# The last batch of expert gates kept in its staging buffer, gate quads spread over more tiles, and rings of four for the rounded activations

## The chip, the cores and the metric

The kernel runs on one core of one Trainium2 chip. The metric is the time of the whole kernel on the device, in microseconds (us). Time before: 3241.5 us, the median of 3 runs (3241.14 to 3247.5).

## The reference

Two decoder layers over 512 tokens of width 1024. Each ends in a mixture of single-neuron experts (128 x 128 = 16384 of them) with 8 retrieval heads that pick 16 experts each for every token. Only this part is touched by the change:

```python
def peer_ffn(h, w_query, sub_keys1, sub_keys2, expert_u, expert_v):
    ...
    gate = jax.nn.softmax(top_v.astype(jnp.float32), axis=-1).astype(h.dtype)
    ...
    def block(args):
        xt, et, gt = args
        act = jax.nn.gelu(jnp.einsum("td,thkd->thk", xt, expert_u[et]), approximate=False) * gt
        return jnp.einsum("thk,thkd->td", act, expert_v[et])
```

## The kernel before

Experts are not gathered for the first 384 of the 512 tokens. For these the kernel computes all experts densely: `a[e, t] = gelu(u_e . h_t) * G[e, t]`, where `G` holds the gates (zero for experts that were not picked), and then `y_t = sum_e a[e, t] v_e`. The last 128 tokens (`FETCHED`) fetch their 128 rows of `u` and `v` each. One layer thus has three stages that matter here.

- **U tiles.** `U` is streamed in 128 tiles (number `n`) of 128 experts. A tile is 24 matmuls on PE (`u_tile`, L948 to L950): 8 slices of the width, each with three products, since weights and activations are split into a rounded high part and a low part. ACT rounds the weight tile (`high`, L500), POOL or DVE subtracts to get the low part (`low`, L437 or L1694), ACT applies gelu (L684) into `gel`, a ring of four, and stores it to DRAM (L688). PE alternates between two banks, so tile `n` waits for the gelu of tile `n - 2`. The last `KEPT = 4` tiles' gelus stay in `gel`.
- **Gates, beside the U tiles from tile `U_EARLY = 26` on.** The gates of four tokens at a time (a quad, 96 of them) are made by DVE's one-hot tiles `hot` and `plane` (L1703, L1708), ACT's low planes (`low_planes`, L723), 4 matmuls on PE (`gate_quad`, L1201), and two adds that put the result in `stage` (`gates_high` on ACT, L733, and `gates_out` on DVE, L1717). `quad_step(q)` says before which of the 8 slices of which tile PE does quad `q`; ACT and DVE take the same table: in tile `n` they finish the quads that PE does there, and prepare the quad two further on. Twelve quads are a batch of 48 tokens. `stage` has two slots of 24 KB in each partition. When a batch is complete, ACT stores it to `g_dram` in four pieces (`store_piece`, L740), one after each of four U tiles; the last batch's four pieces go out together.
- **Rows of the fetched tokens.** POOL fetches rows of `u` (`u_fetch`, L454) and DVE takes the dot product of each with the token (`dot`, L1726), 5 in 4 tiles. Until `U_GATED` POOL also does `low` of tile `n + 2`; from there DVE does.
- **V tiles.** After tile `FIRST_UNIT_AT`, ACT waits until all stored gates have landed and loads the first two units (`load_unit`, L749 and L752): a unit is the gates and the gelus of four tiles. Then, three tiles ahead of PE (`V_AHEAD`), DVE multiplies gelu by gate (`product`, L1754), ACT rounds the product (`a_high`, L760) and DVE subtracts (`a_low`, L1763), into `a_hi` and `a_lo`, rings of 8; PE does 18 matmuls for a V tile (L968). Per V tile DVE also does `low` and adds one fetched row of `v` (L1741).

Every engine works through its own list in order. ACT's list for one U tile, in this order: `high` of tile `n + 3`; for each quad of the tile `gates_high(q)` and `low_planes(q + 2)`; the gelu and its store; a piece of a batch; the first units if it is their turn. DVE's list: for each quad `one_hots(q + 2)` and `gates_out(q)`, then the dots. A wait at the head of a list holds all that is behind it.

## Time and profile before

| | us |
|---|---|
| median of 3 runs | 3241.5 |
| lowest and highest | 3241.14, 3247.5 |
| the profiled execution | 3235.31, span 3233.6 |

PE is busy 95% of the span, DVE 83%, ACT 47%, POOL 50%; the mean granted TensorE clock is 0.979. The DMA engines moved 846.06 MB, 262 GB/s over the span. A view by windows gives each engine's busy time in a stretch, the granted clock and the share of time in which the DMA engines were busy. Rows of waits read "who waited <- for what: us in total, times, longest"; rows of a timeline read start, duration, engine, line, operation, result and sources, and in brackets how long the engine sat idle before and what ended it. The first layer's U tiles with quads run from 565 to 1009 us, its remaining U tiles to 1069, its V tiles to about 1595; the second layer's from 2206 to 2642, to 2701 and to about 3223.

### The profile page before, as it was taken

How to read it: one execution, taken by the hardware profiler on the slowest of the kernel's cores; microseconds unless marked ns; L12 is line 12 of the kernel's file. 1: busy time of each engine (PE TensorE's matmuls, PEld its weight loads, DVE VectorE, ACT ScalarE, POOL GpSimd, SP SyncE). 2: the span in 40 equal slices, each digit the busy share in tenths (PEclk: the TensorE clock that was granted, in tenths of full speed). 3: DMA queues.
4: the chain of work that ended last, by engine and by line, in shares of the span. 5: the costliest groups of instructions: out<-in, count | busy, mean ns of one | idle time of the engine just before them, and what ended most of it. 6: DMA issues, size and time to landing. Idle time of an engine off the chain costs nothing.

```text
span 3233.6 us, 44817 instructions
## 1 busy us (share of the span) xinstructions
PE 3082.8 (95%) x15340; PEld 2681.0 (83%) x15340; DVE 2699.0 (83%) x4632; ACT 1506.1 (47%) x2678; POOL 1617.0 (50%) x880
## 2 busy tenths in 40 slices
PE   4899999999998999999899998999999998999999
PEld 3777799999998888878677667899999997888887
DVE  6676898999997888888875658997999987798887
ACT  3233334666664333333444763346666753333332
POOL 3423345898786443444333004457898884552221
PEclk9899999999999999999999899999999999999999
DMA  5533235899899999999624013257999999999996
GB/s 217 200 134 108 76 115 183 285 343 334 322 317 375 365 368 357 382 360 378 237 79 156 1 39 128 96 164 245 323 345 338 354 355 356 360 366 355 355 351 247
DMA packets 321829, 846.06 MB, mean 262 GB/s; under 512 B 26753, under 2 KB 155793, under 8 KB 321505
## 3 DMA queue, kind: packets, MB, share of 16 engines
q1 hardware_dynamic: 90448, 329.82, 28.7%
q0 software_dynamic: 74000, 268.81, 22.6%
q10 hardware_dynamic: 157184, 244.88, 20.9%
q8 instruction: 117, 1.92, 0.2%
q14 instruction: 80, 0.65, 0.1%
HBM read 742.20 MB, written 101.19 MB: 261 GB/s over the span
## 4 chain that ended last, share of the span: by engine, by line
PE 56%; DVE 19%; POOL 9%; DMA 7%; issue 6%; ACT 1%; ACTq 1%; DVEq 0%; POOLq 0%; SPq 0%
PE banks L968 19%; PE gbank L968 9%; DVE u_rows L1726 7%; POOL w_lo L437 6%; DVE hot L1703 4%; POOL u_rows L454 3%; PE banks L928 3%; PE banks L930 3%; PE banks L929 3%; PE banks L948 3%; PE banks L950 3%; PE banks L949 3%; DMA u_rows<-u_dram,row_of 3%; DVE plane L1708 2%; DVE stage L1717 2%
## 5 line engine op out<-in xcount | busy, mean ns | idle before, releaser
L437 POOL TENSOR_TENSOR w_lo<-raw,w_hi 128x1024 fp32r<-128x1024 f32 x339 | 833.3, 2460 | 783.1 <-ACT w_hi L500 779.8
L500 ACT ACTIVATE w_hi<-raw 128x1024 fp32r<-128x1024 f32 x613 | 648.2, 1058 | 541.0 <-PE banks L968 305.0
L948 PE MATMUL banks<-h_hi,w_hi 128*128 128x384 f32 x2048 | 696.2, 340 | 44.8 <-ACT gel L684 39.1
L462 POOL DMA_INDIRECT v_rows<-v_dram,row_of x256 | 403.4, 1576 | 615.8 <-DVE fetched L1741 599.8
L949 PE MATMUL banks<-h_lo,w_hi 128*128 128x384 f32 x2048 | 688.2, 336 | 0.0
L950 PE MATMUL banks<-h_hi,w_lo 128*128 128x384 f32 x2048 | 688.1, 336 | 0.0
L1726 DVE CUSTOM_DVE_ANT_0 u_rows<-u_rows,h_rows 128x1024 f32<-128x1024 f32 x256 | 462.6, 1818 | 35.6 <-DMA u_rows<-u_dram,row_of 35.5
L454 POOL DMA_INDIRECT u_rows<-u_dram,row_of x256 | 372.1, 1454 | 188.1 <-DVE z L1726 154.1
L948 PEld LDWEIGHTS banks<-h_hi,w_hi 128*128 128x128 f32 x2048 | 387.2, 189 | 61.9 <-issue 46.4
L949 PEld LDWEIGHTS banks<-h_lo,w_hi 128*128 128x128 f32 x2048 | 387.1, 189 | 0.0
L950 PEld LDWEIGHTS banks<-h_hi,w_lo 128*128 128x128 f32 x2048 | 386.7, 189 | 0.0
L1694 DVE TENSOR_TENSOR w_lo<-raw,w_hi 128x1024 fp32r<-128x1024 f32 x274 | 333.8, 1218 | 12.4 <-ACT w_hi L500 12.4
L1741 DVE SCALAR_TENSOR_TENSOR fetched<-v_rows,share,fetched 128x1024 f32<-128x1024 f32 x254 | 326.6, 1286 | 1.2 <-DMA v_rows<-v_dram,row_of 0.7
L723 ACT ACTIVATE plane<-hot,gate_lo 128x128 fp32r<-128x128 f32 x768 | 246.2, 391 | 168.6 <-DVE hot L1703 151.9
L968 PE MATMUL banks<-w_hi,a_lo 128*128 128x512 f32 x1024 | 315.3, 389 | 0.0
L968 PE MATMUL banks<-w_hi,a_hi 128*128 128x512 f32 x1024 | 315.2, 389 | 0.0
L968 PE MATMUL banks<-w_lo,a_hi 128*128 128x512 f32 x1024 | 315.2, 389 | 0.0
L928 PE MATMUL banks<-h_hi,w_hi 128*128 128x512 f32 x696 | 285.2, 410 | 1.4 <-DVE h_lo L1863 1.4
L760 ACT ACTIVATE a_hi<-gin 128x384 fp32r<-128x384 f32 x248 | 129.0, 520 | 330.3 <-DVE gin L1754 324.6
L930 PE MATMUL banks<-h_hi,w_lo 128*128 128x512 f32 x696 | 272.5, 392 | 0.0
L929 PE MATMUL banks<-h_lo,w_hi 128*128 128x512 f32 x696 | 272.5, 392 | 0.0
L1703 DVE TENSOR_TENSOR hot<-banks,exT 128x1024 fp32r<-128x1024 f32 x192 | 233.2, 1215 | 1.0 <-PE gbank L1201 0.9
(320 smaller groups left out, 4862.1 us busy)
## 6 DMA issues: line engine op xcount, KB each, us to landing
raw<-stream_dram SPq DMA_DIRECT2D x613, 512.0 KB
g_dram<-stage ACTq DMA_DIRECT2D x64, 768.0 KB
gates<-g_dram ACTq DMA_DIRECT2D x64, 768.0 KB
gel_dram<-gel ACTq DMA_DIRECT2D x248, 192.0 KB
gin<-gel_dram ACTq DMA_DIRECT2D x62, 768.0 KB
ada_w<-ada_dram ACTq DMA_DIRECT2D x50, 512.0 KB
ada_out<-ada_dram ACTq DMA_DIRECT2D x18, 512.0 KB, 4.6
ada_first<-ada_dram SPq DMA_DIRECT2D x8, 1024.0 KB, 20.0
```

Of the source, the lines that this page charges most:

```text
L437: pool.tensor_tensor(w_lo[:, s, :], raw[:, s, :], w_hi[:, s, :].bitcast(F32), ALU.subtract).then_inc(split_lo, 1)
L454: pool.indirect_dma_start(u_rows[:, j % U_ROWS, :], None, (u0, u1)[layer], bass.IndirectOffsetOnAxis(ap=row_of[:, j:j + 1], axis=0)).then_ ...
L462: pool.indirect_dma_start(v_rows[:, j % V_ROWS, :], None, (v0, v1)[layer], bass.IndirectOffsetOnAxis(ap=row_of[:, j:j + 1], axis=0)).then_ ...
L500: act.activation(w_hi[:, s, :], raw[:, s, :], ACT.Copy).then_inc(split_hi, 1)
L928: pe.matmul(out, wh, hi(k), start=(k == 0), stop=False)
L929: pe.matmul(out, wh, lo(k), start=False, stop=False)
L930: mm = pe.matmul(out, wl, hi(k), start=False, stop=(k == DC - 1))
L948: pe.matmul(out, wh, h_hi[:, k, 0:DENSE_T], start=(k == 0), stop=False)
L949: pe.matmul(out, wh, h_lo[:, k, 0:DENSE_T], start=False, stop=False)
L950: mm = pe.matmul(out, wl, h_hi[:, k, 0:DENSE_T], start=False, stop=(k == DC - 1))
L968: mm = pe.matmul(sums[c][half][:], a, w[:, half * SEQ:(half + 1) * SEQ], start=(v == 0 and a is ah and w is hi), stop=(v == NKEYS - 1 and ...
L1726: dve.tensor_tensor_reduce(row, row, h_rows[:], 1.0, 0.0, ALU.mult, ALU.add, z[:, j:j + 1]).then_inc(S("dotted"), 1)
```

## The change

1. Only the first 7 of the 8 batches are stored and loaded (`STORED`). The eighth stays in slot 1 of `stage`, and `product` becomes two instructions: 336 elements by the loaded gates, and 48 by `stage[:, 1, expert]`. For the first product DVE waits for its own last `gates_out`.
2. To leave slot 1 alone, `gates` and `gin` fit in slot 0 and `a_hi`, `a_lo` move behind `stage`, where the one-hots are before; their rings shrink from 8 to 4.
3. `quad_step` steps by 49/6 slices in place of 15/2. The last quad is in tile 124 in place of 116, so `U_GATED` is 125 in place of 117, and POOL does `low` for 8 more tiles. The batches are complete in tiles 39, 51, 64, 76, 88, 100 and 113 in place of 38, 50, 61, 72, 83, 95, 106 (and 117). Before, tiles 35, 50, 65, 80, 95 and 110 hold two quads each; now none does, and tiles 51 and 100 hold none.
4. The first units are loaded after tile 120 in place of 121, and so while quads still run.

```diff
-A_RING = 8
+A_RING = 4
...
+STORED = NBATCH - 1
+REST = STORED * BATCH
...
-    return QUAD_FROM + 15 * q // 2
+    return QUAD_FROM + 49 * q // 6
...
-FIRST_UNIT_AT = U_GATED + 4
+FIRST_UNIT_AT = NKEYS - 8
...
-    gates = sb("gates", [P, 2, NBATCH, UNIT, BATCH])
+    gates = sb("gates", [P, 2, STORED, UNIT, BATCH])
     gin = sb("gin", [P, 2, UNIT, DENSE_T])
+    place[0] = arena + 2 * NKEYS * BATCH * 4
...
-            batch_at = {quad_step(BATCH_QUADS * b + BATCH_QUADS - 1) // DC + 1: b for b in range(NBATCH)}
+            batch_at = {quad_step(BATCH_QUADS * b + BATCH_QUADS - 1) // DC + 1: b for b in range(STORED)}
...
-                    if n - i in batch_at and (i == 0 or batch_at[n - i] < NBATCH - 1):
+                    if n - i in batch_at:
                         store_piece(batch_at[n - i], i)
-                if batch_at.get(n) == NBATCH - 1:
-                    for i in range(1, PIECES):
-                        store_piece(NBATCH - 1, i)
                 if n == FIRST_UNIT_AT:
                     for s in range(2):
-                        act.wait_ge(S(f"stored{s}"), past[f"stored{s}"] + 16 * PIECES * ((NBATCH + 1 - s) // 2))
+                        act.wait_ge(S(f"stored{s}"), past[f"stored{s}"] + 16 * PIECES * ((STORED + 1 - s) // 2))
...
-                dve.tensor_tensor(x.rearrange("p (b t) -> p b t", b=NBATCH),
-                                  x.rearrange("p (b t) -> p b t", b=NBATCH),
-                                  gates[:, u % 2, :, j, :], ALU.mult).then_inc(S("product"), 1)
+                if n == 0:
+                    dve.wait_ge(S("g_out"), past["g_out"] + QUADS)
+                loaded = x[:, 0:REST].rearrange("p (b t) -> p b t", b=STORED)
+                dve.tensor_tensor(loaded, loaded, gates[:, u % 2, :, j, :], ALU.mult)
+                dve.tensor_tensor(x[:, REST:], x[:, REST:], stage[:, STORED % 2, (n - KEPT) % NKEYS, :],
+                                  ALU.mult).then_inc(S("product"), 1)
```

The lines of the kernel after are numbered 1 to 4 higher from here on. DVE's list at the first tile with two quads (tile 35; `hot` and `plane` prepare a quad, `stage` finishes one, the rows named u_rows and z are a dot), before:

```order
L1703 TENSOR_TENSOR hot<-banks,exT 128x1024
L1708 TENSOR_TENSOR plane<-hot,banks 128x4x128
L1717 TENSOR_TENSOR stage<-stage,gbank 128x128x4
L1703 TENSOR_TENSOR hot<-banks,exT 128x1024
L1708 TENSOR_TENSOR plane<-hot,banks 128x4x128
L1717 TENSOR_TENSOR stage<-stage,gbank 128x128x4
L1726 ISA u_rows,z<-u_rows,h_rows 128x1024
L1726 ISA z 128x1
```

The same place now:

```order
L1704 TENSOR_TENSOR hot<-banks,exT 128x1024
L1709 TENSOR_TENSOR plane<-hot,banks 128x4x128
L1718 TENSOR_TENSOR stage<-stage,gbank 128x128x4
L1727 ISA u_rows,z<-u_rows,h_rows 128x1024
L1727 ISA z 128x1
L1704 TENSOR_TENSOR hot<-banks,exT 128x1024
L1709 TENSOR_TENSOR plane<-hot,banks 128x4x128
L1718 TENSOR_TENSOR stage<-stage,gbank 128x128x4
```

The second quad has moved behind the dots, into the next tile.

ACT's list around the load of the first units, from the `high` of tile 121 on, before:

```order
L500 ACTIVATE w_hi<-raw 128x1024
L684 ACTIVATE gel<-banks 128x384
L688 DMA gel_dram<-gel 128x384
L749 DMA gates<-g_dram 128x8x192 x2
L752 DMA gin<-gel_dram 128x4x384
L500 ACTIVATE w_hi<-raw 128x1024
L684 ACTIVATE gel<-banks 128x384
```

Now, from the quad of tile 120 on:

```order
L737 ACTIVATE stage<-gbank 128x128x4
L727 ACTIVATE plane<-hot,gate_lo 128x128 x4
L688 ACTIVATE gel<-banks 128x384
L692 DMA gel_dram<-gel 128x384
L753 DMA gates<-g_dram 128x7x192 x2
L756 DMA gin<-gel_dram 128x4x384
L504 ACTIVATE w_hi<-raw 128x1024
L737 ACTIVATE stage<-gbank 128x128x4
L727 ACTIVATE plane<-hot,gate_lo 128x128 x4
L688 ACTIVATE gel<-banks 128x384
```

The three loads now stand in front of a tile with a quad: its two quad steps (`stage`, `plane`) are behind the loads and ahead of the gelu that PE waits for.

## Rows read from the trace of the kernel before

**Rows 1.** Windows: us, each engine's busy us (and instructions), granted clock, DMA share, GB/s.

```profile
565.00:1009.00 444.00, 427.73 (x2526) 419.94 (x2525) 432.83 (x504) 296.35 (x654) 374.28 (x200) 0.99 0.91 323
1009.00:1069.00 60.00, 49.08 (x264) 47.68 (x263) 36.27 (x49) 17.67 (x25) 25.70 (x17) 0.91 0.96 367
1069.00:1592.00 523.00, 520.34 (x2293) 430.29 (x2294) 441.83 (x548) 194.55 (x256) 224.94 (x131) 1.00 0.96 366
2206.00:2642.00 436.00, 424.88 (x2529) 416.37 (x2528) 426.13 (x504) 296.69 (x654) 377.28 (x200) 1.00 0.92 329
2642.00:2701.00 59.00, 48.23 (x262) 46.86 (x260) 35.68 (x49) 17.15 (x25) 25.18 (x17) 0.91 0.97 371
```

**Rows 2.** Timeline of PE: three gate quads in tiles 102, 103 and 104.

```profile
939.38 0.64 PE L1201 MATMUL gbank<-plane,hot 128*128 128x256 f32 x4
943.50 0.64 PE L1201 MATMUL gbank<-plane,hot 128*128 128x256 f32 x4
948.14 0.64 PE L1201 MATMUL gbank<-plane,hot 128*128 128x256 f32 x4
```

**Rows 3.** Waits of PE from 565 to 1009 us, the largest.

```profile
PE banks L948 <- ACT gel L684: 11.9, 9, 3.4
```

**Rows 4.** Waits of PE from 2206 to 2642 us, the largest.

```profile
PE banks L948 <- ACT gel L684: 8.5, 9, 2.6
```

**Rows 5.** Timeline of ACT in tile 35, the first with two quads.

```profile
606.53 1.28 ACT L723 ACTIVATE plane<-hot,gate_lo 128x128 fp32r<-128x128 f32 x4 [1.82 <-issue]
```

**Rows 6.** Timeline of PE behind it.

```profile
610.78 0.41 PE L948 MATMUL banks<-h_hi,w_hi 128*128 128x384 f32 x1 [1.35 <-ACT gel L684]
```

**Rows 7.** Waits of PE from 990 to 1075 us.

```profile
PE banks L948 <- ACT gel L684: 9.2, 1, 9.2
PE banks L948 <- DVE w_lo L1694: 1.0, 1, 1.0
```

**Rows 8.** Waits of PE from 2620 to 2706 us.

```profile
PE banks L948 <- ACT gel L684: 9.5, 1, 9.5
```

**Rows 9.** Timeline of ACT around the first units of the first layer.

```profile
1031.87 0.34 ACTq L688 DMA_DIRECT2D gel_dram<-gel  x1
1034.71 7.21 ACTq L749 DMA_DIRECT2D gates<-g_dram  x2
1041.94 5.39 ACTq L752 DMA_DIRECT2D gin<-gel_dram  x1
```

**Rows 10.** Timeline of ACT later, the load of one unit among the V tiles.

```profile
1107.81 0.37 ACTq L749 DMA_DIRECT2D gates<-g_dram  x1
1108.21 0.61 ACTq L752 DMA_DIRECT2D gin<-gel_dram  x1
```

**Rows 11.** DMA queues from 1034 to 1048 us, ACT's own: packets, MB, share of 16 engines.

```profile
q10 hardware_dynamic: 1150, 1.16, 23.2%
```

**Rows 12.** Timeline of ACT: the gelu of tile 102.

```profile
944.64 0.47 ACT L684 ACTIVATE gel<-banks 128x384 f32<-128x384 f32 x1
```

**Rows 13.** Windows, columns as in rows 1: the first 5 us after the stall.

```profile
1049.00:1054.00 5.00, 4.99 (x16) 5.00 (x17) 5.00 (x7) 2.49 (x3) 2.24 (x2) 0.50 1.09 396
```

**Rows 14.** Timeline of DVE: two dots in tile 102.

```profile
944.65 1.98 DVE L1726 CUSTOM_DVE_ANT_0 u_rows<-u_rows,h_rows 128x1024 f32<-128x1024 f32 x1
...
946.56 1.22 DVE L1726 CUSTOM_DVE_ANT_0 u_rows<-u_rows,h_rows 128x1024 f32<-128x1024 f32 x1
```

**Rows 15.** Timeline of POOL at that time.

```profile
943.12 2.42 POOL L437 TENSOR_TENSOR w_lo<-raw,w_hi 128x1024 fp32r<-128x1024 f32 x1
945.70 1.76 POOL L454 DMA_INDIRECT u_rows<-u_dram,row_of  x1 [0.16 <-issue]
```

**Rows 16.** The product's line: duration in ns, least, median and most.

```profile
L1754 DVE TENSOR_TENSOR gin<-gin,gates x248: 545/551/560, 1075.8 to 3206.5; 128x384 f32<-128x384 f32 x124
```

**Rows 17.** Timeline of DVE: the nearest small multiply, 96 elements.

```profile
1073.09 0.25 DVE L1734 TENSOR_TENSOR share<-share,z 128x96 f32<-128x96 f32 x1
```

**Rows 18.** Waits of PE from 1069 to 1600 us, the largest.

```profile
PE gbank L968 <- DVE w_lo L1694: 2.5, 1, 2.5
```

More of the change, by code:

```diff
@@ L115 @@
 COUNTS = {"scores": N_WQ, "sc": N_WQ, "ranked": N_WQ, "gate_arg": 1, "gate_exp": 1, "ex": 3, "ex_tp": 3,
-          "exT": 5, "hot": QUADS, "one": QUADS, "one_lo": QUADS, "gate_lo": 1, "g_mm": QUADS, "g_hi": QUADS, "g_out": QUADS, "stored0": 16 * PIECES * ((NBATCH + 1) // 2), "stored1": 16 * PIECES * (NBATCH // 2), "picked": 2,
+          "exT": 5, "hot": QUADS, "one": QUADS, "one_lo": QUADS, "gate_lo": 1, "g_mm": QUADS, "g_hi": QUADS, "g_out": QUADS, "stored0": 16 * PIECES * ((STORED + 1) // 2), "stored1": 16 * PIECES * (STORED // 2), "picked": 2,
           "h_rows": 1, "h_copied": 1, "v_row": 16 * PICKS // V_ROWS, "dotted": PICKS, "z_gel": 2,
@@ L328, in build @@
     fetched = sb("fetched", [P, D])
-    g_dram = [nc.dram_tensor(f"g_dram{l}", (NBATCH, P, NKEYS, BATCH), F32, kind="Internal").ap()
+    g_dram = [nc.dram_tensor(f"g_dram{l}", (STORED, P, NKEYS, BATCH), F32, kind="Internal").ap()
               for l in range(2)]
```

## The prediction

> **What bounds the kernel now.** I read the windows by stage first. In the V tiles PE is busy 520.3 of 523 us at full clock [rows 1]: PE alone bounds them, and the DMA engines' 96% and DVE's 442 us are cover that is almost used up but still covers. The waits of PE say so too: one of 2.5 us in the first layer's V tiles [rows 18]. The two stretches of U tiles are where time can move: 444 and 436 us for tiles 27 to 116, 60 and 59 us for the rest [rows 1].
>
> What would PE alone need? The quads at 939.38, 943.50 and 948.14 are 7 and then 8 slices apart [rows 2]: 4.12 and 4.64 us. So a slice (3 matmuls) is 0.52 us, a tile 4.16, a quad 4.12 - 7 x 0.52 = 0.48. Ninety tiles with 96 quads are 374.4 + 46.1 = 420.5 us. The stretches took 444 and 436: 23.5 and 15.5 us over. The eleven tiles behind are 45.8 us of matmuls in 60 and 59 us: 14.2 and 13.2 over. These four excesses, 66.4 us in all, are what the change can touch; the rest of the kernel is as it was.
>
> **Part 1: no tile with two quads.** In tile 35 ACT's first plane of a quad starts 1.82 us late, since DVE has two quads' one-hots to make in one tile and ACT's gelu stands behind both planes; PE then waits 1.35 us for that gelu [rows 5, 6]. PE waited for a gelu 9 times in each stretch, 11.9 and 8.5 us [rows 3, 4]. By their times those behind tiles 35, 50, 65, 80, 95 and 110 add up to 5.9 us in each layer. Each such wait costs a little more than it shows, since the first matmul behind it takes 0.41 us where it starts the next after 0.17 when PE runs on; with about 8 waits that is 1.9. Sum: 7.8 us in a layer. Some would remain (the wait at tile 65 has a late fetched row in it too), so I take 7.5 off, between 4 and 9. The quads themselves are not removed: 96 x 0.48 is paid in either table. What is late next is the loop of POOL and DVE: POOL's low part, then a fetch, then the next low part [rows 15]: 2.42 + 0.16 + 1.76 is 4.34 in a tile with one dot, and one tile in four has a second dot, 1.22 us at the least [rows 14]: 4.65 on average, against PE's 4.64. So the cover behind PE is thin, and what I take off cannot be more than the 9.
>
> **Part 2: the last batch's store goes.** After tile 117 its four pieces crowd the DMA engines; PE waits 1.0 us for a low part whose weights came late [rows 7]. Off: 1.0 in a layer, down to nothing if it was chance. The seven other batches are stored as before, only 12.25 tiles apart in place of 11.25, so their collisions with late rows stay: no change, with 3 us to either side in a layer, since they fall on other tiles.
>
> **Part 3: the first units.** Before, ACT ended tile 121 at 1032.2, waited 2.5 us for the store to land, and then was held by three loads for 7.21 + 5.39 = 12.6 us; PE stood for 9.2 us [rows 7, 9], 9.5 in the second layer [rows 8]. (a) The wait for the store goes: the last stored piece now leaves after tile 116, four tiles earlier. That is 2.5 off. (b) The loads still hold ACT. One unit later on costs 0.37 + 0.61 us [rows 10], so not the issue itself is slow but the queue is full: gates are 1024 pieces of 768 bytes, gin 512. In 14 us the queue passed 1150 packets [rows 11], 82 in a us; 12.6 us are 1030, the size of one load of gates. I read it as: the third load gets in when as much as the first one has left. Three loads are now 896 + 896 + 512, 256 fewer: 12.6 - 256 / 82 = 9.5 us, 3.1 off. Bounds: nothing off (the hold is a time and no count), and 7 us left (the queue drains faster, with no store before it). (c) Against it, the place is worse. Where quads run, ACT's gelu lags: tile 103's quad is at slice 3 and at 943.50, so tile 102 had ended at 941.9, and its gelu came at 944.64 [rows 2, 12], 2.7 us late, where after tile 121 it was at once. Behind the loads ACT now does a stage copy and four planes ahead of the gelu: 0.6 + 1.3. PE's two tiles of slack are longer by two quads: 1.0. Sum: 9.2 - 2.5 - 3.1 + 2.7 + 1.9 - 1.0 = 7.2 us, 2.0 less than before, between 5 and 10, the bounds of (b). (d) After the stall PE runs at 0.50 of its clock (the 1.2 GHz level) for 16 matmuls in 5 us [rows 13], 2.3 us lost; that stays. (e) DVE stands too, at the stage add of tile 121, while PE's list behind has three more quads. I add 1.0 for it, between 0 and 3.
>
> **Part 4: eight tiles more with POOL's low part.** A dot beside POOL's subtraction takes 1.98 us, and one beside a fetch 1.22 [rows 14, 15]: in tiles 117 to 124 ten dots are 7.6 us longer, but DVE no longer makes these tiles' low parts, and at one quad a tile it keeps PE's pace as it does in tiles 51 to 113. PE pays at most 0.03 a tile by that loop, and I add 0.3 for a stray wait: 0.5 in a layer, between 0 and 3. The Trainium skill (SBUF — State Buffer, on the pair of ports that DVE and GpSimd share) says that a DVE instruction with two SBUF inputs and a GpSimd one that reads SBUF exclude each other for the whole instruction; the 1.98 beside 1.22 agrees with it.
>
> **Part 5: the V tiles.** The product of 384 elements takes 0.551 us [rows 16]; the nearest small multiply, 96 elements, 0.25 [rows 17]. Two instructions for one cost between 0 and 0.25 us more; I take 0.1, 12 us of DVE's time in a layer, where DVE is idle for 523 - 442 = 81 [rows 1]. Off the path. The unit's gates are 96 KB less, and land sooner. The only spot where DVE was late is the 2.5 us [rows 18]: 0, between -2.5 and +3. The Trainium skill (VectorE: DVE Perf Modes, the TRN2 errata on a fixed latency per instruction) speaks against the split: by its formula for an fp32 tensor_tensor, (N + 151) cycles at 0.96 GHz, the two are 0.16 us more than the one; by it DVE would lose 20 us in a layer, still inside the 81. The rings of four cost nothing: ACT rounds product v + 3 only behind its weight rounding, which has already waited for PE's tile v - 1.
>
> **Sum** in a layer: -7.5 - 1.0 - 2.0 + 1.0 + 0.5 = -9.0 us; two layers -18.0. By its own time the profiled execution would go from 3235.3 to 3217.3; the median shown is 6.2 above that execution, and I forecast against it: 3241.5 - 18.0 = 3223.5 us.
>
> **The rivals.** (A) The quads' stalls move and do not go. The two-quad waits are what pays, and with so thin a cover the POOL and DVE loop may be late elsewhere, once a fetched row is late. Then -7.5 becomes -2, and the stall at the loads stays as long as it was: -2 - 1.0 + 1.0 + 0.5 = -1.5 a layer, 3238.5. For it: DVE is busy 433 of 444 us; against it: the long waits stand exactly behind the two-quad tiles in both layers. (B) The queue takes the three loads at once, since they are fewer: PE's stall goes with its slow clock, another 7.2 + 2.3 + 1.0 a layer: 3202.5. Against it: in the first layer two loads, 2048 pieces, were already held for 7.2 us [rows 9], and now the three are 2304. (C) Slower. The loads come while DVE still has quads and dots; rows arrive late, and ACT's planes wait for DVE in each tile from 121 to 124, and DVE comes into the V tiles behind. Its price: the worst gelu wait among the quads, 3.4 us [rows 3] with another 2.3 of slow clock [rows 13], once or twice in a layer; with Part 1 half paid and Part 3 at nothing: -4 - 1.0 + 1.0 + 5.7 x 1.5 + 0.5 = +5.1 a layer, 3251.7. It decides from the point where DVE is more than 12.5 us (the three tiles 125 to 127) behind PE at tile 124. Against it: behind the quads DVE is busy for only 36 of 60 us [rows 1], so it catches up fast. (D) The change does nothing at the loads and the two-quad waits were no more than 4: near A.
>
> **Chances.** Forecast 0.70, with its own range 3212 to 3233; A (with D) 0.17; B 0.06; C 0.07. A measurement of this kernel can tell about 0.2% (6.5 us) from no change. Faster than 3235: the forecast, B and a small part of A: 0.76. Same: 0.17. Slower: 0.07. The range takes in A's time and leaves out most of B and C: 3211 to 3240.
>
> **What the profile after would show.** PE's waits for a gelu from 565 us to tile 124: under 7 us in a layer, and none behind tiles 35, 50, 80, 95 and 110; the gelus of these tiles 4.3 to 5.6 us apart like their neighbours. The three loads after tile 120 hold ACT for 9 to 10 us, with no wait in front, and PE stands once for about 7 us, then 16 or so matmuls at 0.50. V begins about 9 us earlier, counted from the first quad. The V tiles take 523 us again. It would be wrong if PE's waits in tiles 26 to 116 are as long as before (A), or PE waits more than once behind tile 120 (C), or not at all (B).

## The result

The kernel after takes 3202.2 us (median of 4 runs, 3198.4 to 3210.0) beside 3244.5 us (3241.1 to 3261.4) for the kernel before on the same chip: ratio 0.986, 95% interval 0.984 to 0.989, some 44 us less. On another chip it came to 0.989 (0.986 to 0.993). The forecast was 18 us less, and the time lies below its range. Ratios here are of fast runs alone; the one slow run among all kernels took 6172 us (e10_before_ring4 below), and why is not known. The profiled execution of after took 3201.2 us, with a mean granted clock of 0.982 in place of 0.979.

Windows of the kernel after by stage, columns as in [rows 1]: the first layer's U tiles with quads up to the loads of the first units, the rest of its U tiles, its V tiles, and the two U stretches of the second layer.

```profile
559.00:1010.00 451.00, 441.89 (x2641) 437.03 (x2641) 431.65 (x510) 299.43 (x654) 401.34 (x210) 1.00 0.92 333
1010.00:1044.00 34.00, 28.73 (x159) 28.13 (x159) 28.03 (x35) 15.72 (x28) 24.37 (x14) 0.95 0.93 326
1044.00:1582.00 538.00, 528.62 (x2304) 435.62 (x2304) 455.59 (x680) 196.67 (x259) 262.55 (x130) 0.99 0.94 352
2191.00:2633.00 442.00, 438.66 (x2632) 435.29 (x2631) 422.82 (x509) 298.84 (x651) 404.49 (x210) 1.00 0.94 339
2633.00:2667.00 34.00, 30.46 (x168) 29.56 (x166) 27.65 (x36) 16.23 (x31) 25.48 (x15) 0.95 0.95 337
```

From the first quad to the first V tile it is 484.7 and 476.3 us, before 505.3 and 496.4: some 20 us less in each layer, not 9. Against that the first layer's V tiles, forecast at 523 again, take 538.7 after and 526.6 before; the second layer's take 523.4 in both. Another 4.4 us came ahead of the first quad (563.7 and 559.3 us), where no instruction differs; later executions of either kind start their quads anywhere from 557 to 566 us, so this is chance.

Waits of PE in the kernel after, columns as in [rows 3]: U tiles up to the loads, U tiles from there, V tiles; then the second layer's U tiles in the same two parts.

```profile
PE banks L949 <- ACT gel L688: 6.8, 3, 2.6
...
PE banks L949 <- ACT gel L688: 3.8, 1, 3.8
...
PE gbank L969 <- DVE w_lo L1695: 8.7, 4, 3.3
...
PE banks L949 <- ACT gel L688: 2.4, 1, 2.4
...
PE banks L949 <- ACT gel L688: 2.3, 1, 2.3
```

The nine waits for a gelu among the quads in each layer [rows 3, 4] are three and one, as forecast. The stall of 9.2 and 9.5 us at the loads [rows 7, 8] was to be 7.2; it is 3.8 and 2.3. What DVE's low parts cost in the V tiles has grown from 2.5 us [rows 18] to 8.7.

ACT's timeline of after at the loads, the first layer, then the second. Rows of ACTq are DMA issues; their duration is how long the issue kept ACT.

```profile
1010.07 1.21 ACTq L753 DMA_DIRECT2D gates<-g_dram  x2
1011.31 4.28 ACTq L756 DMA_DIRECT2D gin<-gel_dram  x1
...
2634.56 1.12 ACTq L753 DMA_DIRECT2D gates<-g_dram  x2
2635.71 0.71 ACTq L756 DMA_DIRECT2D gin<-gel_dram  x1
...
2639.64 3.94 ACTq L692 DMA_DIRECT2D gel_dram<-gel  x1
```

Three loads held ACT for 12.6 us before [rows 9]. Now it is 5.5 us in the first layer; in the second the loads go in within 1.9 us, and the next gelu's store is held for 3.9. The first load starts 0.6 us behind the gelu's store: ACT no longer waits for stored gates.

The queues of after from 1010 to 1016 us: packets, MB, share of 16 engines.

```profile
q10 hardware_dynamic: 1036, 0.87, 45.8%
q0 software_dynamic: 68, 0.22, 9.4%
```

ACT's queue q10 passed 1036 packets in 6 us, 173 in a us, where it had passed 82 [rows 11]. Before, q0, which brings the fetched rows, had 52.9% of the engines in the 14 us of [rows 11]; here it has 9.4%.

PE's clock behind the stall, two windows of after: the last 3 us of the stall and the 5 us behind.

```profile
1016.00:1019.00 3.00, 0.09 (x1) 0.12 (x2) 1.74 (x2) 2.77 (x7) 2.17 (x1) 1.00 1.04 386
1019.00:1024.00 5.00, 5.00 (x22) 5.00 (x23) 4.97 (x8) 3.62 (x8) 1.12 (x2) 0.66 1.05 409
```

After 3.8 us idle the clock is at 0.66 over 5 us, where 9.2 us idle had brought 0.50 [rows 13]: 22 matmuls in place of 16. In the second layer 2.3 us idle brought 0.66 from 2648 to 2653 us as well. While PE was at work the slow clock cost 2.5 us before (5 us at 0.50) and 1.7 after (5 us at 0.66).

### The profile page after: what moved, and what is told of

Its sections match the earlier page's. It is cut to its first block, busy times and chain, and to the rows that moved or that the text cites. A ratio compares the mean times of both kernels' runs of the same rounds, so it can differ in the third digit from the quotient of the medians.

```text
span 3199.2 us, 45065 instructions
## 1 busy us (share of the span) xinstructions
PE 3071.2 (96%) x15340; PEld 2678.8 (84%) x15340; DVE 2703.6 (85%) x4872; ACT 1504.9 (47%) x2678; POOL 1653.5 (52%) x896
## 4 chain that ended last, share of the span: by engine, by line
PE 51%; POOL 23%; issue 9%; DVE 9%; DMA 7%; ACT 1%; ACTq 0%; POOLq 0%; DVEq 0%; SPq 0%
PE banks L969 17%; POOL w_lo L441 14%; POOL u_rows L458 9%; PE gbank L969 8%; DMA ada_w<-ada_dram 4%; PE banks L929 3%; PE banks L931 3%; PE banks L930 3%; DVE u_rows L1727 2%; PE banks L950 2%; PE banks L951 2%; PE banks L949 2%; DMA u_rows<-u_dram,row_of 2%; DVE w_lo L1695 1%; DVE hot L1704 1%
## 5 line engine op out<-in xcount | busy, mean ns | idle before, releaser
L441 POOL TENSOR_TENSOR w_lo<-raw,w_hi 128x1024 fp32r<-128x1024 f32 x355 | 870.4, 2454 | 775.9 <-ACT w_hi L504 769.9
L466 POOL DMA_INDIRECT v_rows<-v_dram,row_of x256 | 390.4, 1525 | 645.6 <-DVE fetched L1742 630.3
L458 POOL DMA_INDIRECT u_rows<-u_dram,row_of x256 | 384.6, 1502 | 95.3 <-DVE z L1727 52.6
L1695 DVE TENSOR_TENSOR w_lo<-raw,w_hi 128x1024 fp32r<-128x1024 f32 x258 | 314.0, 1217 | 0.0
## 6 DMA issues: line engine op xcount, KB each, us to landing
gin<-gel_dram ACTq DMA_DIRECT2D x62, 768.0 KB, 13.3
```

The lines of the kernel that those rows point to most:

```text
L441: pool.tensor_tensor(w_lo[:, s, :], raw[:, s, :], w_hi[:, s, :].bitcast(F32), ALU.subtract).then_inc(split_lo, 1)
L458: pool.indirect_dma_start(u_rows[:, j % U_ROWS, :], None, (u0, u1)[layer], bass.IndirectOffsetOnAxis(ap=row_of[:, j:j + 1], axis=0)).then_ ...
L466: pool.indirect_dma_start(v_rows[:, j % V_ROWS, :], None, (v0, v1)[layer], bass.IndirectOffsetOnAxis(ap=row_of[:, j:j + 1], axis=0)).then_ ...
```

## The experiments

For each profiled execution I took two excesses: the time between the gelus of two tiles, less 4.16 us a tile and 0.48 a quad, the needs of PE worked out in the prediction. One is over tiles 27 to 116, the other over 116 to 127, where the loads are. "Gelu" means its start on ACT. "U" is first quad to first V tile, "V1" the first layer's V tiles. Two numbers are the two layers. Ratios are to the kernel before, with 95% intervals.

| kernel | ratio | U | excess 27 to 116 | excess 116 to 127 | V1 |
|---|---|---|---|---|---|
| before | 1 | 505.3, 496.4 | 24.2, 15.8 | 13.6, 13.1 | 526.6 |
| before_again | 1.000 (0.998 to 1.003) | 500.0, 497.7 | 19.2, 17.5 | 13.3, 12.7 | 535.7 |
| after | 0.986 (0.984 to 0.989) | 484.7, 476.3 | 13.9, 6.7 | 3.3, 2.1 | 538.7 |
| after_again | 0.989 (0.986 to 0.993) | 480.8, 478.4 | 10.8, 8.5 | 2.5, 2.4 | 531.4 |
| e1_old_spread | 0.992 (0.990 to 0.995) | 490.7, 497.3 | 17.4, 21.7 | 5.7, 8.0 | 532.2 |
| e5_burst | 0.999 (0.997 to 1.001) | 497.6, 500.3 | 18.4, 19.0 | 11.6, 13.7 | 544.6 |
| e9_burst_no_wait | 0.999 (0.997 to 1.001) | 502.8, 496.4 | 20.8, 14.6 | 14.3, 14.2 | 537.8 |
| e4_two_quads | 0.987 (0.983 to 0.991) | 483.9, 486.5 | 13.7, 15.6 | 2.6, 3.4 | 541.4 |
| e6_twelve_two_quads | 0.993 (0.990 to 0.996) | 482.3, 487.2 | 15.5, 17.3 | -0.8, 2.4 | 539.5 |
| e8_every_tile | 0.988 (0.985 to 0.992) | 483.3, 474.2 | 9.2, 5.5 | 6.4, 1.2 | 543.0 |
| e2_one_product | 0.987 (0.983 to 0.990) | 477.4, 478.5 | 9.9, 11.3 | 0.0, -0.3 | 527.1 |
| one_product_again | one run, 3212.3 us | 484.6, 488.4 | 14.7, 18.2 | 2.3, 2.7 | 535.8 |
| e3_dot_later | 0.982 (0.978 to 0.987) | 481.4, 489.4 | 9.2, 16.0 | 4.7, 5.9 | 524.9 |
| e7_split_loads | 0.985 (0.981 to 0.988) | 480.8, 478.6 | 10.8, 11.5 | 2.5, -0.5 | 525.0 |
| before_split_loads | 0.998 (0.996 to 1.000) | 501.9, 492.4 | 23.1, 13.4 | 11.3, 11.4 | 533.8 |
| e10_before_ring4 | 1.000 (0.998 to 1.003) | 505.8, 499.5 | 24.2, 18.2 | 13.9, 13.8 | 542.8 |
| e11_before_dot_later | 0.995 (0.994 to 0.997) | 499.6, 500.1 | 18.4, 19.2 | 13.7, 13.4 | 523.4 |
| e12_sum | 0.982 (0.979 to 0.984) | 477.1, 468.0 | 10.1, 3.3 | -0.6, -2.9 | 525.0 |

One execution's U tiles differ by several us from the next with the same program, so means count. In tiles 27 to 116 the old table's eight kernels (the two of before, e1, e5, e9, before_split_loads, e10, e11) have a mean excess of 19.1 us a layer, the 49/6 table's six (the two of after, e2, e3, e7, one_product_again) one of 11.8: 7.3 us less, with some 2.5 to either side by their scatter.

These two excesses have a fault: they end at the gelu of tile 116, and how late that gelu is depends on the table. The old table has no more quads to prepare there, so ACT runs the gelu 0.2 us behind PE's end of the tile in all 16 layers; with the new table it comes 2.8 to 6.9 us behind. First PE's quad in tile 115 before and in tile 116 after, then the gelus of tile 116, before and after:

```profile
1002.07 0.63 PE L1201 MATMUL gbank<-plane,hot 128*128 128x256 f32 x4
...
980.00 0.64 PE L1202 MATMUL gbank<-plane,hot 128*128 128x256 f32 x4
```

```profile
1008.95 0.49 ACT L684 ACTIVATE gel<-banks 128x384 f32<-128x384 f32 x1 [1.49 <-PE banks L950]
...
990.44 0.47 ACT L688 ACTIVATE gel<-banks 128x384 f32<-128x384 f32 x1
```

So I also took the excess on PE itself, by its quads: from the first quad to the last one up to slice 931 (slice 925 with the old table, 930 with the new, both about tile 116), less 0.52 us a slice and 0.48 a quad, and from there to the first V tile. Means over the layers:

| kernels | first quad to tile 116 | tile 116 to V |
|---|---|---|
| before's order: old table, a last store, loads after tile 121 (before, before_again, e5, e9, e10, e11; 12 layers) | 21.6 | 14.4 |
| e1_old_spread: old table, no last store, loads after tile 120 | 22.0 | 7.8 |
| after's order: new table, no last store, loads after tile 120 (after, after_again, e2, e3, one_product_again; 10 layers) | 9.6 | 8.3 |
| e4_two_quads | 14.9 | 6.2 |
| e6_twelve_two_quads | 17.2 | 3.4 |
| quads every 8 slices (e8_every_tile, e12_sum) | 6.5 | 5.0 |

The split moves: up to tile 116 the new table saves 11.8 us a layer (21.5 in the old table's eight kernels, 9.7 in the new one's six; 2.3 to either side), and from there to V the change saves 6.2 (2.2 to either side), where the gelus gave 7.3 and 10.8. The sum is the same 18. PE's idle time up to tile 116 fell from 13.0 to 5.7 us a layer, and its waits of any length from 17 to 6.

### The table and the last store

Theory: the new table makes most of the gain. Rival: that the last batch is not stored does.

```diff
-    return QUAD_FROM + 49 * q // 6
+    return QUAD_FROM + 15 * q // 2
```

> The changed kernel with the old table of quads (steps of 15/2 slices: six tiles with two quads, last quad in tile 116), the rest of the change kept: seven batches stored, loads after tile 120. Theory 1 (the spread pays by having no tile with two quads, the missing store pays at the loads): 8 to 10 us a layer come back in tiles 27 to 120, so about 3218 us; the loads hold ACT for 5 to 6 us, as in the changed kernel, and PE stands for less than 4 us there. Theory 2 (the spread is worth nothing, all of the gain is the store that went): 3200 to 3204 us. Theory 3 (all of it is the spread): PE stands 7 us or more at the loads again, 3235 or more.

The old table gives back about half of the gain. Its excess up to tile 116 is that of before. Behind it the excess stays some 6 us below before. The burst was put back onto this kernel, in four pieces behind the last quad, with ACT's wait for it ahead of the loads:

```diff
-FIRST_UNIT_AT = NKEYS - 8
+FIRST_UNIT_AT = NKEYS - 7
...
+                if n == U_GATED:
+                    act.wait_ge(S("g_out"), past["g_out"] + QUADS)
+                    for i in range(PIECES):
+                        own = slice(i * NKEYS // PIECES, (i + 1) * NKEYS // PIECES)
+                        act.dma_start(burst_dram[layer][:, own].rearrange("p e t -> p (e t)"),
+                                      stage[:, STORED % 2, own, :].rearrange("p e t -> p (e t)")
+                                      ).then_inc(S("burst"), 16)
                 if n == FIRST_UNIT_AT:
+                    act.wait_ge(S("burst"), past["burst"] + 16 * PIECES)
```

> The changed kernel with the old table of quads, and with the eighth batch stored after tile 117 in four pieces at once, to a tensor that nobody reads, and waited for in front of the first loads, which are after tile 121: so all is as in the kernel before, but for the loads of seven batches (2304 pieces of data, not 2560) and the split product. Theory R (the loads are held for a count of packets, and what changed is the rate at which ACT's queue drains, since after a burst of stores the late rows take the DMA engines): the loads hold ACT for 8 to 11 us again and PE stands 6 to 9 us in a layer; 12 us more than with the old table of quads alone, 3236 to 3244. Theory C (the fewer pieces alone do it): they hold ACT for 5 us, PE stands less than 5 us, 3226 to 3232.

With table, store and the place of the loads as before, the time is that of before, and so is nearly the stall (8.4 and 9.2 us). These three are the change, as far as time goes; the 256 fewer pieces to load and the split product aren't told from nothing. To see whether the wait or the hold makes the stall, the same kernel had the wait moved behind the U tiles:

> The kernel of run e5_burst (old table, eighth batch stored in four pieces behind tile 117, units loaded after tile 121) without ACT's wait for that store ahead of the loads; the wait stands behind the U tiles now. There the wait was 3 us and the three loads held ACT for 12.3 and 11.7 us, and PE stood 8.4 and 9.2. Theory (the queue lets ACT go when so many packets have left, whatever they are): the loads enter a queue that still holds the rest of the store, so they hold ACT longer by what the wait was, 14 to 16 us in all; PE stands 8 to 9.5 us as in e5_burst, U tiles 497 to 500 us, the whole time the same within 0.3%. Rival (the forecast's sum: wait and hold add up): the hold stays at 12, PE stands 5.5 to 6.5 us, U tiles 494 to 497 us, 5 us off the whole time.

ACT's loads in e5_burst (first layer), then in e9_burst_no_wait (both layers):

```profile
1025.20 4.61 ACTq L755 DMA_DIRECT2D gates<-g_dram  x2
1029.84 7.69 ACTq L758 DMA_DIRECT2D gin<-gel_dram  x1
```

```profile
1029.23 8.04 ACTq L755 DMA_DIRECT2D gates<-g_dram  x2
1037.30 6.91 ACTq L758 DMA_DIRECT2D gin<-gel_dram  x1
...
2674.25 1.06 ACTq L755 DMA_DIRECT2D gates<-g_dram  x2
2675.34 14.21 ACTq L758 DMA_DIRECT2D gin<-gel_dram  x1
```

12.3 us of hold behind a wait became 15.0 and 15.3 without one, PE stood 9.3 and 9.7 us (8.4 and 9.2 in e5_burst), and the time is the same. So while the store is in the queue, wait and hold are one thing: without the wait ACT spends the same time on the issue. It does not say that the store makes the hold: in e5_burst the store had landed before the loads were issued, and they were held for 12.3 and 11.7 us all the same.

In e1_old_spread, with no store in the queue, the loads held ACT like this, first layer and second:

```profile
1020.19 1.31 ACTq L753 DMA_DIRECT2D gates<-g_dram  x2
1021.52 7.93 ACTq L756 DMA_DIRECT2D gin<-gel_dram  x1
...
2660.79 1.20 ACTq L756 DMA_DIRECT2D gin<-gel_dram  x1
...
2663.56 11.30 ACTq L692 DMA_DIRECT2D gel_dram<-gel  x1
```

Four tiles behind the last quad the holds are still 9.2 us, and 2.8 and then 11.3 (PE stands 3.8 and 6.1 us), with q10 at 140 packets in a us from 1021 to 1030 and 91 from 2660 to 2675, and q0 at 39 to 47% of the engines. My expectation was 5 to 6 us of hold and under 4 of stall, so Theory 1 held only in part. From tile 116 to V the excess is 14.4 us with the store and its wait, 7.8 without them, and 8.3 in after's order, where the loads stand beside the quads. So by this the 6.2 us there go with the store and the wait for it, and the place beside the quads cost next to nothing. That rests on the two layers of e1_old_spread, 6.7 and 8.9.

Nor is the hold of 5.5 us in after's first layer the rule for this program. In eight of the ten layers with after's order the three loads went in within 2.5 us, and in four of these eight the next store of a gelu was then held, for 2.4 to 6.9 us; PE stood for 0 to 5.2 us, 1.8 on average, where it stood for 8.4 to 10.7 in the twelve layers with before's order. ACT's loads in after_again, first layer:

```profile
1013.17 1.33 ACTq L753 DMA_DIRECT2D gates<-g_dram  x2
1014.52 0.82 ACTq L756 DMA_DIRECT2D gin<-gel_dram  x1
```

In all kernels with the new table q0 had 3 to 43% of the engines while the loads went in, in those with the old one 36 to 53%. Why the fetched rows leave more room beside the quads isn't shown; that PE asks for a weight tile every 4.64 us there and every 4.16 behind the quads is only argued.

### What in the table pays

Theory: the tiles with two quads. They were put back into the new table alone, by moving the quads of six tiles one tile ahead, then of twelve:

```diff
-    return QUAD_FROM + 49 * q // 6
+    step = QUAD_FROM + 49 * q // 6
+    if step // DC in TWO_QUADS:
+        step = step // DC * DC - 1
+    return step
+
+
+TWO_QUADS = (36, 45, 66, 81, 90, 111)
```

> The changed kernel with six quads moved back to the last slice of the tile in front (tiles 36, 45, 66, 81, 90 and 111 lose theirs to the tile before), so that six tiles have two quads again, while the last quad is still in tile 124. Theory 1 (a tile with two quads costs PE 1.3 to 1.6 us): 8 to 10 us a layer, 3218 to 3222. Theory 2 (such tiles cost nothing, fewer quads in a tile on average is what pays): 3200 to 3205.

> The changed kernel with twelve tiles of two quads (the quads of tiles 31, 36, 41, 45, 58, 66, 73, 81, 86, 90, 104 and 111 in the last slice of the tile in front), twice the dose of the run with six. Theory 1 (1.3 to 1.6 us for each such tile): 16 to 19 us a layer more than the changed kernel, 3233 to 3240. Theory 3 (about 0.6 us each, as the run with six says within its noise): 7 us a layer, 3216 to 3220. Theory 2 (nothing): 3202.

> The kernel after with one thing changed: the quads' table steps by 8 slices in place of 49/6, so that every tile from 27 on has exactly one quad and the last is in tile 122. By the five earlier executions with the new table, tiles 27 to 116 take 11 us more than PE's matmuls need, with the old table 19, and with six or twelve tiles of two quads put into the new one 15 to 16. Theory: two-quad tiles make up half of the difference and the denser table (7.5 slices a quad, so 1.25 dots and more than one quad to a tile for DVE) the other half. 8 slices is as free of two-quad tiles as the new one and three quarters as wide: 11 to 14 us over in tiles 27 to 116, U tiles 480 to 487 us, whole time within 0.3% of the kernel after (ratio to before 0.985 to 0.990). Rival: only the two-quad tiles count; then 9 to 12 us over, and the U tiles as after. Rival: the rare tile without a quad (two in the new table) is where a late DVE gets back; without any, a delay is never caught up: over 17 us, U tiles over 488.

Waits of PE among the quads, first layer: e6_twelve_two_quads, then e12_sum (a quad every 8 slices, below) in the second layer.

```profile
PE banks L955 <- ACT gel L694: 8.3, 8, 3.7
```

```profile
PE banks L950 <- ACT gel L688: 0.9, 1, 0.9
PE banks L950 <- POOL w_lo L441: 0.2, 1, 0.2
```

Behind each tile with two quads the next gelu comes late, in every execution: with the old table 2.8 us over PE's need at tiles 35 and 95 and about 1.7 at 50, 65, 80 and 110. Yet the tiles that follow get part of it back. By PE's quads, six such tiles raise the excess up to tile 116 from 9.7 to 14.9 us and twelve to 17.2: 0.6 to 0.9 us each, where the forecast's list of waits had 1 to 1.3, from one execution of each, and one layer differs from the next by 2.7 us (one standard deviation). In the whole time the six don't show (0.987, beside 0.986 and 0.989 of after), the twelve do (0.993). So the old table's six make some 4 to 5 us of the 11.8. What the rest is stays open. By place, 3.1 us of the 11.8 lie ahead of tile 60, 7.1 in tiles 60 to 90 and 1.6 behind. That fewer quads in a tile pay would fit, but it is argued and not shown: with a quad every 8 slices, a little denser than the new table, the excess is 6.5 us and not more (e8_every_tile was expected at 11 to 14 by the gelus, and had 9.2 and 5.5). A tile without a quad isn't needed for catching up.

A rival that no run tests is where the stores of the seven other batches fall. In tiles 74 to 98 PE waits over 1.9 us for a gelu 30 times, 20 in the old table's 16 layers and 10 in the new one's 12, each time three to five tiles behind a batch's last piece. Ahead of every one of them a fetched row lands 1.3 to 2.4 us late for DVE, and its dot takes 3.1 to 4.2 us. In this one, of before's first layer, ACT's planes then wait for DVE, and PE for the gelu behind them.

```profile
870.45 3.82 DVE L1726 CUSTOM_DVE_ANT_0 u_rows<-u_rows,h_rows 128x1024 f32<-128x1024 f32 x1 [1.57 <-DMA u_rows<-u_dram,row_of]
...
875.45 1.28 ACT L723 ACTIVATE plane<-hot,gate_lo 128x128 fp32r<-128x128 f32 x4 [4.18 <-DVE hot L1703]
...
877.24 0.66 PE L948 MATMUL banks<-h_hi,w_hi 128*128 128x384 f32 x1 [2.61 <-ACT gel L684]
```

In tile 90 it stands in 14 of the old table's 16 layers; with the new one in tiles 94 and 95 in 4 of 12. The new table moves these stores, so it changes more than the number of quads in a tile.

### The V tiles of the first layer

The first layer's V tiles hold dots of DVE with rows of conditioning weights (`ada_w`), one in seven tiles. Waits of DVE in them, after and then before:

```profile
DVE ada_w L1321 <- DMA ada_w<-ada_dram: 52.6, 9, 9.7
```

```profile
DVE ada_w L1320 <- DMA ada_w<-ada_dram: 27.9, 5, 8.0
```

ACT issues the load right behind a unit's load, 1.3 us after its `gin`; it lands 17 us later, and DVE stands 9.1 us for it. From after's timelines of ACT and of DVE:

```profile
1131.33 0.75 ACTq L756 DMA_DIRECT2D gin<-gel_dram  x1
1132.61 0.49 ACTq L531 DMA_DIRECT2D ada_w<-ada_dram  x1
```

```profile
1131.95 0.50 DVE L1758 TENSOR_TENSOR gin<-gin,gates 128x336 f32<-128x336 f32 x1
1132.37 0.20 DVE L1759 TENSOR_TENSOR gin<-gin,stage 128x48 f32<-128x48 f32 x1
1132.49 1.28 DVE L1742 SCALAR_TENSOR_TENSOR fetched<-v_rows,share,fetched 128x1024 f32<-128x1024 f32 x1
...
1150.01 1.23 DVE L1321 CUSTOM_DVE_ANT_0 ada_w<-ada_w,cvec 128x1024 f32<-128x1024 f32 x1 [9.10 <-DMA ada_w<-ada_dram]
```

My first reading was that the split product eats the time in which DVE catches up. One product again, all 384 elements by `stage` (whose slots are adjacent), and, on its own, the dot two tiles later:

```diff
-                dve.tensor_tensor(loaded, loaded, gates[:, u % 2, :, j, :], ALU.mult)
-                dve.tensor_tensor(x[:, REST:], x[:, REST:], stage[:, STORED % 2, (n - KEPT) % NKEYS, :],
+                dve.tensor_tensor(whole, whole, spare, ALU.mult)
...
-                if layer == 0 and v % 7 == 2 and v // 7 < V_DOTS:
+                if layer == 0 and v % 7 == 4 and v // 7 < V_DOTS:
```

> The changed kernel with one product instruction of 384 elements for each V tile, that reads all its gates from the slot of the last batch (wrong gates; the loaded units are still loaded and not used). Only DVE's time differs: one instruction of 0.55 us for two of 0.50 and 0.20. Theory V1 (the first layer's V tiles became 12 us longer since the second instruction took DVE's time to catch up between waits for ada_w): PE's waits for w_lo in the first layer's V tiles go from 8.7 us to 0 to 3, and the kernel is 5 to 9 us faster, 3193 to 3197. Theory V2 (the transfers of ada_w land later, whatever DVE does): no change, 3202.

> The changed kernel with the dot of each ada_w row in V tile 7i + 4 in place of 7i + 2, two tiles (8 us) later, the load in the same place. Theory V1 and V2 both say that DVE then finds ada_w landed (it waited up to 9.8 us for it): the V tiles of the first layer go from 539 us back to 523 to 527, and the kernel to 3187 to 3192. If the V tiles are long for another reason (gin late, or a ring of four), they stay at 535 or more, 3198 or more.

In V1 both gave what that reading wanted (527.1 and 524.9 us). Their median times did not: 3203.3 us for one product, as Theory V2 had it, and 3200.2 for the later dot, where 3187 to 3192 was expected. The reading fell by further executions and by controls on the kernel before:

> The kernel before, unchanged, for a second profiled execution. Theory (the late load of conditioning weights holds DVE in before as in after, by chance more or less): first layer's V tiles 532 to 545 us, DVE waits 45 to 65 us in all for that load, PE waits 6 to 14 us for DVE's low parts. Rival (the split product is what makes the V tiles longer): 524 to 529 us, and DVE's waits near the 27.9 us of the first execution.

> The kernel of run e2_one_product (after, with one product of 384 elements; the last batch's gates are left wrong by it) for a second profiled execution. Theory (the split has no part in it): the first layer's V tiles are now 530 to 543 us, as in the kernel after. Rival (the split is the cause): 524 to 528 us, as in e2_one_product's first execution (527.1).

> The kernel before with one thing changed: the rings of the rounded activations are 4 in place of 8. Theory: ACT rounds product v + 3 only behind its weight rounding, which has waited for PE's tile v - 1, so a ring of four never holds it: the same time within 0.3%, V tiles 523 to 527 us in the first layer and 523 to 524 in the second. Rival: the ring of four takes part in the 12 us that the first layer's V tiles are longer in the kernel after; then they are over 530 us here.

> The kernel before with one thing changed: the dot that DVE does on a row of the conditioning weights among the first layer's V tiles comes two tiles later (every seventh tile, at v = 4 modulo 7 in place of 2). Theory: the load behind it queues behind a unit's load and lands late; before, PE waited 2.5 us for it once, and that goes: V tiles of the first layer 523 to 525 us, 2 to 3 us off, which the ratio can hardly show (0.998 to 1.001). Rival: before, that wait had another cause (DVE behind from the U tiles); V tiles 526 to 527.

Waits in the first layer's V tiles: e10_before_ring4's PE and DVE; e11_before_dot_later's DVE, where none for `ada_w` is left.

```profile
PE gbank L968 <- DVE w_lo L1694: 12.3, 4, 4.4
...
DVE ada_w L1320 <- DMA ada_w<-ada_dram: 60.0, 8, 9.2
```

```profile
DVE a_lo L1763 <- ACT a_hi L760: 40.6, 63, 1.1
DVE gin L1754 <- DMA gin<-gel_dram: 24.6, 10, 5.1
```

With before's product, V1 was 535.7 us in before_again (DVE waited 43.0 us for `ada_w`, a little under what I expected), 533.8 in before_split_loads and 542.8 with the rings of four; with one product again it was 535.8. So the late load stretched these tiles before the change too, and the 526.6 of the first profile was at the low end by luck. The later dot takes 0.5% off the kernel before (0.995), as it does off after (0.982 beside 0.986 and 0.989), and V1 is 523.4 to 525.0 in all four kernels with it. Whether the split costs anything stays open: kernels with one product have 533.6 us on average (six executions), with two 538.6 (eight), 5.0 apart, with 6.0 to either side. The rings of four changed nothing in the time.

### The loads alone, and the sum

Splitting the loads (unit 0 after tile 119, unit 1 after 121, with the later dot) and the same in the kernel before (after 121 and 123):

```diff
-                    for u in range(2):
-                        load_unit(u)
+                    load_unit(0)
+                if n == FIRST_UNIT_AT + 2:
+                    load_unit(1)
```

> The changed kernel once more, as it is, beside the others of this job: its profile shows how much the U tiles of one and the same kernel differ between executions. So far three kernels with the same U tiles took 476 to 489 us from the first quad to the first V tile. Expected: 3200 to 3206 us, U tiles 476 to 489, V tiles of the first layer 536 to 541.

> The changed kernel with the ada_w dots two V tiles later, and with the first two units loaded apart: the first (896 pieces) after tile 119, the second (1408) after tile 121. If the hold is a matter of how much is in the queue, no load holds ACT for more than 1.5 us, PE has no wait over 2 us at tiles 121 to 124, and 3 to 5 us a layer go: 3177 to 3186 us. If the hold is there whatever the split, 3184 to 3190.

> The kernel before with one thing changed: the two first units are not loaded together after tile 121, but the first after tile 121 and the second after tile 123. Theory (ACT is held until the queue has passed some 1000 packets beyond what it takes at once): one load of gates, 1024 pieces of 768 bytes, goes in in 1 to 3 us behind the landed store, the second finds the queue partly drained and is held for 0 to 6; PE stands 0 to 4 us in place of 9.2, U tiles 488 to 495 us a layer in place of 501 (mean of the old table's executions), ratio to before 0.992 to 0.997. Rival (the wait for the store and the place after tile 121 make the stall, not the count): PE stands 7 to 9 us, ratio 0.999 to 1.001.

ACT's issues around the loads, e12_sum (first layer, split as in e7_split_loads), then before_split_loads:

```profile
1015.66 1.37 ACTq L756 DMA_DIRECT2D gin<-gel_dram  x1
...
1019.08 1.85 ACTq L692 DMA_DIRECT2D gel_dram<-gel  x1
```

```profile
1030.70 3.66 ACTq L688 DMA_DIRECT2D gel_dram<-gel  x1
...
1036.31 1.72 ACTq L749 DMA_DIRECT2D gates<-g_dram  x1
1038.06 7.86 ACTq L752 DMA_DIRECT2D gin<-gel_dram  x1
```

In the kernel before, splitting only deals the hold out over three issues (13.2 us in all): PE still stands 6.7 and 7.7 us, and the time falls by 0.2%, against my expectation of 0.3 to 0.8. Behind the new table and without the store, it leaves no hold over 1.1 us in e7_split_loads; but its time (3193.8 us, expected 3177 to 3186) isn't told from that of e3_dot_later. The three edits that held went into one kernel:

> The kernel after with the three edits together that held one by one: quads every 8 slices, the first unit loaded after tile 119 and the second after tile 121, and the conditioning dot two tiles later. Theory (they add up): tiles 27 to 116 take 5 to 11 us more than PE needs, no load or store holds ACT for over 2 us, U tiles 474 to 482 us, V tiles of the first layer 524 to 525; ratio to before 0.980 to 0.984. Rival (quads stand closer to the loads' place now and their last is in tile 122, so what the table gives is lost at the loads): U tiles over 482, ratio 0.985 or more.

The time is the expected one: 3186.1 us (5 runs, 3178.3 to 3193.0) beside 3246.5, and PE's waits in its second layer's U tiles are the 1.1 us shown above. It is faster than both kernels of this case. Whether all three edits add to it isn't shown by the time, for e3_dot_later alone has 0.982 too (0.978 to 0.987).

## Why the prediction was wrong

Two steps failed, and both made the forecast too small: the cap that Part 1 put on the table's gain (at most 9 us, measured 11.8), and the price that Parts 3 and 4 put on the place beside the quads (5.1 us, measured 0.5).

**Part 1** (-7.5 a layer, at most 9) measured -11.8, by PE's quads up to tile 116. That two-quad tiles cost PE time was right, but they account for some 4 to 5 us. The term was sized by PE's waits for gelus, nine in a layer, at 0.24 us more for each of eight. PE's waits of any length were 17 in a layer and are 6; its idle time fell by 7.3 us, and the rest is matmuls that run slower behind a wait, part of it by the clock: 0.74 over 10 us behind before's longest wait, 3.4 us at 810 us. The waits behind late rows, which the sum took as unchanged, were 1.25 a layer in tiles 74 to 98 and are 0.83. Where in the table the other 7 us come from stays open. The loop of POOL and DVE with its thin cover did not turn on the change, which speaks against rival A.

**Parts 2 to 4** (-1.0 - 2.0 + 1.0 + 0.5 = -1.5 a layer from tile 116 to V) measured -6.2.
- What goes with the store was sized well, in part by luck: -2.5 in (a), -3.1 in (b) and -1.0 in Part 2 are -6.6, and e1_old_spread, which has no store and the old table, is 6.6 below before's order. But the 3.1 were for 256 fewer pieces, and e5_burst, which has these fewer pieces and the store, is no faster than before.
- The place beside the quads was to cost (c) 2.7 + 1.9 - 1.0, (e) 1.0 and 0.5 in Part 4, 5.1 in all. It cost 0.5: 8.3 in after's order beside 7.8 in e1_old_spread. This is the step that failed here. The gelu does lag there, but the loads are held for less, 1.8 to 5.5 us, which the sum left out; how much of one is set off against the other isn't shown.
- (b) "12.6 - 256 / 82 = 9.5 us" took the rate from before, where the queue shared the engines with fetched rows at half their time. It holds for e1_old_spread's first layer (9.2 us) and not for after: 173 packets in a us and 5.5 us of hold in the first layer. The count isn't sound either. About 1030 packets had passed when ACT was let go before and 1036 from 1010 to 1016 us in after, but in after_again 239 passed while the same three loads went in, and e1_old_spread's queue passed 1262 and 1370 in the 9 and 15 us of its holds. What sets the hold stays open. The lower bound, 7 us left, named the faster queue but gave it no rate.
- (d) "After the stall PE runs at 0.50 of its clock ... that stays" was near: 2.5 us lost before, 1.7 after.

**Part 5** (0 a layer, from -2.5 to +3) was outside its bounds in the profiled execution, +12.1 in the first layer, but most of that is not the change's: the one execution of before on which [rows 18] rests had V tiles 7 to 16 us shorter than three later ones with the same product (533.8, 535.7, 542.8). Rings of four at nothing held. The split product's price in the path is open, 5 us with 6 to either side.

**Sum.** 11.8 + 6.2 is 18 us a layer, as the U tiles of the kernels with either order differ on average (500.1 and 482.0), so 36 us for two, and the ratios give 34 to 44. Rival B, which had the queue take the loads at once, gave 3202.5 us with a chance of 0.06. It named the right side of the error, and in eight of ten layers the loads did go in within 2.5 us; that its sum came out at the measured time is luck, since it left Part 1 at 7.5 and PE still stood. Rivals A and C did not happen.

## What to carry to other kernels

When an issue holds an engine, take the rate of its DMA queue from what will share the engines at the new place and not from the old one, and give the hold a wide range: one and the same program had 2 and 5.5 us. A wait ahead of such an issue isn't a term of its own while the same store stands in the queue. Measure a stretch on the engine that bounds it: its end in another engine's time moved 4.5 us from one part of this account to the other. One profiled execution shows a stage with late transfers at one draw of luck: before a stage is called unchanged or longer, look at a second execution of the same kernel. And check where a small load is issued behind a large one on the same queue: moving its use by two tiles was worth 0.5% here, splitting the large ones alone 0.2%.

## What the runs showed of the hardware

- 2304 pieces of loads went into ACT's queue in 1.8 to 5.5 us in the kernels with after's order, and in 2.8 and 9.2 us in e1_old_spread. ACT was then often held a few us later, on a store of one gelu tile: 3.9 us in after's second layer, 11.3 in e1_old_spread's. So a hold can show at the next issue, though that one is small.
- The queue's rate in such a hold went with the fetched rows' share of the engines: 77 packets in a us at 51.5% (before, 2667 to 2680 us), 82 at 52.9% [rows 11], 91 at 47.4% and 140 at 39.4% (e1_old_spread), 173 at 9.4% and 242 at 26.0% (after, 1010 to 1016 and 2639 to 2644 us).
- Two vector products of 336 and 48 elements take 0.50 and 0.20 us by their own durations, but from start to start 0.42 + 0.12, since they overlap; the one of 384 elements took 0.551 [rows 16]. From start to start the two need 0.54 us where the one needed 0.47 in before's timeline, less than the 0.1 us that I took for the split.
- The granted clock behind a stall of PE: 0.66 in the 5 us behind 3.8 us and behind 2.3, 0.50 behind 9.2. Of these 9.2 us the last 5 were at 0.50 already, with PE idle, so they cost nothing more.
- A dot of DVE that started 0.33 us ahead of a subtraction of POOL (2.40 us), because its row was late, took 3.82 us (before, at 870 us), where the same dot takes 1.98 and 1.22 in [rows 14].
